# Turning joined with scoring, and the last stage's query factor and gate products rearranged, in a ten-stage transformer kernel

## The chip, the cores and the metric

The kernel runs on one core of one Trainium2 chip. The metric is the device time of one execution in microseconds (us). A measurement of a kernel is several executions; their median is given.

## The reference, cut to what matters

Two blocks are run one behind the other on 512 rows of width 1024, in float32. The first has two layers of a gated feed-forward, a mix of a short convolution and a forgetting attention over 8 heads of 64, a cross attention to 256 memory rows, and a second feed-forward. The second block is one layer of differential attention (8 heads, two score maps each) and one of stick-breaking attention with 16 heads of 64:

```python
z = jnp.einsum('bhqd,bshd->bhqs', qb, k).astype(jnp.float32) * scale
log_beta = jax.nn.log_sigmoid(z)
log_1mb = jnp.where(mask, jax.nn.log_sigmoid(-z), 0.0)
suffix = lax.cumsum(log_1mb, axis=3, reverse=True) - log_1mb
a = jnp.where(mask, jnp.exp(log_beta + suffix), 0.0)
...
proj = _rms(x, norm_g) @ w_in
q, g = jnp.split(proj, [SB_W], axis=-1)
o = _stick_breaking(q.reshape(b, s, SB_HEADS, SB_HEAD_DIM), k, v)
return x + (o.reshape(b, s, SB_W) * jax.nn.silu(g)) @ w_out
```

The norm of a row x is one factor per row, 1/sqrt(mean(x^2) + eps), times a gain per column.

## The kernel before

Ten stages follow one another: feed-forward, mix, cross attention, feed-forward, the same four again, `diff` and `sb` (the last). Activations stand as columns (128 features on the partitions, 512 rows along the free axis). Each matrix product is done in three passes for float32 accuracy: every operand is split into a high half (ScalarE, L1872 and L1875 for weights) and a low half (VectorE, L2255 for weights), and `mm3` (L1525 to L1527) issues low x high, high x low, high x high. A tile of 128 output features takes 8 such steps of 3 products of 512 columns. Weights come in blocks of 128x1024; in the last stage GpSimd first multiplies them by a gain (L2783).

The attention of a stage is laid into the projections. `att(n0, n1)` runs over n, where n = 4t + i is query block i (128 rows) of head pair t. A step of `bs`, `ms` or `ds` is the score product (L1770; six matmuls of 64 partitions into banks 4 and 5, over 128 x (i + 1) keys), with what follows on ScalarE and VectorE; a step of `bt` or `dt` turns the finished probabilities of block m = n - 2 (n - 3 in the last stage) by TensorE transposes (L1531; 2 x (i + 1) blocks into banks 6 and 7, in `diff` i + 1 blocks), after which ScalarE copies the high half (L2179) and VectorE subtracts the low half (`btl`, L2711; `dtl`, L2644). A turn waits for that subtraction of the turn before it. When all four blocks of a head pair are turned, the value products follow (`bpv`, L1811 and L1812; two per pair, one per pair in `diff`). Between steps the generator yields. `weave` advances this side stream by a fixed rate for each unit of 256 columns of the main stream: 10.5/80 means 10.5 side steps while 80 units of projection are issued. `later(5, ...)` puts a step on the other engines' order after 5 more units; `due` puts it there at once. One list, `order`, is the program order of every engine.

In the last stage a score becomes two sigmoids (ScalarE, L2170 with scale -1 and L2171), a reversed running product per head (VectorE scans, L2701), a masking product (L2705), and a product on GpSimd (L2889). Queries and keys are multiplied in their bank by RB, the rows' norm factors (VectorE, `bqe`, L2687), then copied (ScalarE, L2160) and subtracted (VectorE, `bql`, L2693). The output of a head pair stands in two banks, one per head, each in its own 64 partitions: `bps` (L2471) adds the half that `bpv` moved, `gy` (L2730) multiplies each half by the gate in ET, and L2187 and `gl` (L2736) split the result. The gate is made by `ga` (L2718), a sigmoid (L2183) and `gb` (L2723). In `diff`, column sums for the norms are small products (L1726, after ScalarE's squares L2097 and L2102; L1623, after L2145).

## Time and profile before

| | |
|---|---|
| Median of 3 runs (lowest, highest) | 2911.08 us (2909.06, 2913.7) |
| The profiled execution: its time, its span | 2911.05 us, 2909.2 us |
| Busy: TensorE, VectorE, ScalarE, GpSimd | 2843.3, 1676.3, 1092.2, 397.3 us |
| Mean granted TensorE clock | 0.995 of full |
| Instructions | 34967 |

The span goes from the first to the last instruction. Matmuls are pipelined, so their durations overlap and the start-to-start distance is what one costs. "Waits" name for each idle stretch of an engine the instruction that ended it.

### The profile page before, as it was taken

The numbers are of one execution on the slowest core, as the hardware profiler recorded it, in microseconds if no ns is written. First come the engines' busy times: TensorE is split into PE (matmuls) and PEld (weight loads), VectorE is DVE, ScalarE is ACT, GpSimd is POOL, SyncE is SP. The second block draws the span as 40 slices with busy tenths as digits, with TensorE's granted clock in tenths as the row PEclk, the third lists the DMA queues.
The fourth block names the chain that finished last, engine by engine and source line by source line (L and its number), as shares of the span: only waits on it lengthen the run. The fifth ranks groups of instructions, "written<-read, shape, count | busy, mean of one in ns | idle before, by whom it ended". The sixth has DMA issues, their size and how long they took to land.

```text
span 2909.2 us, 34967 instructions
## 1 busy us (share of the span) xinstructions
PE 2843.3 (98%) x14241; PEld 2363.5 (81%) x14241; DVE 1676.3 (58%) x2400; ACT 1092.2 (38%) x1699; POOL 397.3 (14%) x263
## 2 busy tenths in 40 slices
PE   8999999999999999999999999999999899899988
PEld 7888887888888888888887889888888787678777
DVE  5554357675464533555247776555533677768884
ACT  4322244554332322323234454422222444444442
POOL 2000111110100001000011220100001322154430
PEclk9999999999999999999999999999999999999999
DMA  4332332243233233332323233233323222131211
GB/s 141 101 95 94 95 88 73 66 127 106 87 94 97 88 101 98 101 95 87 105 71 92 68 108 118 80 109 95 101 91 98 70 64 69 47 88 59 72 59 51
DMA packets 302240, 258.08 MB, mean 89 GB/s; under 512 B 11367, under 2 KB 299904, under 8 KB 302080
## 3 DMA queue, kind: packets, MB, share of 16 engines
q1 hardware_dynamic: 300704, 254.76, 28.7%
q8 instruction: 113, 1.85, 0.3%
q10 hardware_dynamic: 1024, 1.05, 0.2%
q14 instruction: 47, 0.39, 0.0%
q0 software_dynamic: 352, 0.03, 0.0%
HBM read 252.66 MB, written 2.10 MB: 88 GB/s over the span
## 4 chain that ended last, share of the span: by engine, by line
PE 82%; DVE 10%; ACT 3%; issue 3%; POOL 2%; DMA 1%; ACTq 0%; SPq 0%; POOLq 0%; DVEq 0%
PE PS L1525 26%; PE PS L1527 25%; PE PS L1526 25%; DVE WL L2255 3%; PE PS L1531 2%; PE PS L1770 1%; DVE AF L2701 1%; DVE SM L2619 1%; ACT AF L2129 0%; PE PS L1623 0%; PE PS L1812 0%; PE PS L1811 0%; DVE AR L2711 0%; ACT WH L1872 0%; POOL SM L2869 0%
## 5 line engine op out<-in xcount | busy, mean ns | idle before, releaser
L2255 DVE TENSOR_TENSOR WL<-RAW,WH 128x1024 fp32r<-128x1024 f32 x480 | 617.9, 1293 | 572.9 <-ACT WH L1872 572.6
L1525 PE MATMUL PS<-XH,WL 128*128 128x512 f32 x2256 | 904.4, 401 | 2.9 <-DVE XL L2265 2.9
L1527 PE MATMUL PS<-XH,WH 128*128 128x512 f32 x2256 | 883.3, 392 | 0.0
L1526 PE MATMUL PS<-XL,WH 128*128 128x512 f32 x2256 | 882.1, 391 | 0.0
L1872 ACT ACTIVATE WH<-RAW 128x1024 fp32r<-128x1024 f32 x448 | 465.4, 1044 | 1005.9 <-PE PS L1527 994.6
L1525 PEld LDWEIGHTS PS<-XH,WL 128*128 128x128 f32 x2256 | 425.8, 189 | 101.5 <-issue 12.7
L1527 PEld LDWEIGHTS PS<-XH,WH 128*128 128x128 f32 x2256 | 425.2, 188 | 91.5
L1526 PEld LDWEIGHTS PS<-XL,WH 128*128 128x128 f32 x2256 | 426.3, 189 | 81.1
L1525 PE MATMUL PS<-AR,WL 128*128 128x512 f32 (+1 forms) x1216 | 465.3, 383 | 7.3 <-DVE SC L2599 3.5
L1527 PE MATMUL PS<-AR,WH 128*128 128x512 f32 (+1 forms) x1216 | 460.7, 379 | 0.0
L1526 PE MATMUL PS<-AR,WH 128*128 128x512 f32 (+1 forms) x1216 | 460.6, 379 | 0.0
L2805 POOL TENSOR_TENSOR SC<-SC 128x512 f32<-128x512 f32 x70 | 117.5, 1678 | 1619.3 <-ACT SC L1897 1614.7
L1525 PEld LDWEIGHTS PS<-AR,WL 128*128 128x128 f32 x1216 | 229.4, 189 | 52.0 <-issue 9.2
L1527 PEld LDWEIGHTS PS<-AR,WH 128*128 128x128 f32 x1216 | 229.2, 188 | 43.1
L1526 PEld LDWEIGHTS PS<-AR,WH 128*128 128x128 f32 x1216 | 229.4, 189 | 41.0
L1525 PE MATMUL PS<-WH,XL 128*128 128x256 f32 x384 | 113.3, 295 | 0.8 <-DVE AR L2693 0.8
L2324 DVE TENSOR_TENSOR AF<-PS,RB 128x512 f32<-128x512 f32 x88 | 60.4, 687 | 85.9 <-PE PS L1527 85.9
L1526 PE MATMUL PS<-WL,XH 128*128 128x256 f32 x384 | 109.1, 284 | 0.0
L1527 PE MATMUL PS<-WH,XH 128*128 128x256 f32 x384 | 109.0, 284 | 0.0
L2337 DVE TENSOR_TENSOR AR<-AF,AR 128x512 fp32r<-128x512 f32 x88 | 60.9, 692 | 61.7 <-ACT AR L1934 61.7
L2318 DVE TENSOR_TENSOR SC<-PS,RB 128x512 f32<-128x512 f32 x88 | 60.1, 687 | 59.1 <-PE PS L1527 45.6
L1934 ACT ACTIVATE AR<-AF 128x512 fp32r<-128x512 f32 x88 | 55.3, 628 | 98.5 <-DVE AF L2332 98.5
(259 smaller groups left out, 3000.0 us busy)
## 6 DMA issues: line engine op xcount, KB each, us to landing
RAW<-in_w_ffn_gu_dram SPq DMA_DIRECT2D x176, 512.0 KB, 3.5
RAW<-in_w_ffn_down_dram SPq DMA_DIRECT2D x80, 512.0 KB, 3.4
RAW<-in_w_mix_in_dram SPq DMA_DIRECT2D x48, 512.0 KB, 4.0
RAW<-in_w_xkv_dram SPq DMA_DIRECT2D x32, 512.0 KB, 3.4
RAW<-in_a_w_in_dram SPq DMA_DIRECT2D x32, 512.0 KB, 4.2
RAW<-in_w_mix_out_dram SPq DMA_DIRECT2D x16, 512.0 KB, 3.4
RAW<-in_w_xq_dram SPq DMA_DIRECT2D x16, 512.0 KB, 4.1
RAW<-in_w_xo_dram SPq DMA_DIRECT2D x16, 512.0 KB, 3.4
```

The source lines that it names most:

```text
L1525: pe.matmul(o, ll, rh, start=start, stop=False, skip_group_check=skip)
L1526: pe.matmul(o, lh, rl, start=False, stop=False, skip_group_check=skip)
L1527: return pe.matmul(o, lh, rh, start=False, stop=stop, skip_group_check=skip)
L1531: t = pe.transpose(PS[b][:, i * 128:(i + 1) * 128], src[:, i * 128:(i + 1) * 128], ID)
L1770: w = pe.matmul(PS[4 + hh][:, 0:N], QK[r, q, qs], QK[r, k, 0:N], start=q == sl + 1, stop=last and q == sl and k == sl + 2)
L1872: act.activation(h, src, ACT.Copy).then_inc(sg["wh"].up(n))
L1934: act.activation(AH[:, f, :], AF[:, (f % 2) * T:(f % 2) * T + T], ACT.Copy).then_inc(sg["fh"].up(s, f))
L2255: dve.tensor_tensor(l, raw_slot(n), F(h), ALU.subtract).then_inc(sg["wl"].up(n))
L2318: dve.tensor_tensor(S[f % 2], PS[C.banks[f % 2]][:, :], RB[:, :], ALU.mult).then_inc(sg["fs"].up(s, f))
L2324: dve.tensor_tensor(w, PS[C.banks[f % 2]][:, :], RB[:, :], ALU.mult).then_inc(sg["fu"].up(s, f))
L2337: dve.tensor_tensor(AL[:, f, :], AF[:, (f % 2) * T:(f % 2) * T + T], F(AH[:, f, :]), ALU.subtract).then_inc(sg["fl"].up(s, f))
L2805: pool.tensor_tensor(S[5], S[5], square_of(m), ALU.add).then_inc(sg["acc"].up(s, m))
```

## The change

Turning is joined with scoring: in the four attention stages the generator no longer yields between a turn and the score that follows it, and the rates of the side streams are set anew for the smaller number of steps. In the last stage the queries are taken from their bank without the norm factor; it goes in as the scale per row of the two sigmoids (RCOL, and NB4 = -RCOL, made once). `bps` of the second head writes into the bank of the first, so that one product of 128 partitions (`gy`) serves both heads, and the second bank is free once it is added.

```diff
@@ mix, att (the same in diff and sb with n >= 32)
                     self.add("bt", (s, m), "ptr", "ph")
-                    yield
+                    if n >= 16:
+                        yield
@@ mix
-        side = self.stream(att(0, 4), 6.5 / 64)
+        side = self.stream(att(0, 4), 4.3 / 64)
...
-            side = self.stream(att(4 * m, 4 * m + 4), 10.5 / 80)
+            side = self.stream(att(4 * m, 4 * m + 4), 6.3 / 80)
...
-        side = self.stream(att(12, 16), 10.5 / 80)
+        side = self.stream(att(12, 16), 6.3 / 80)
@@ diff
-            side = self.stream(att(4 * t, 4 * t + 4), 9.4 / (80 if t in (2, 4) else 48))
+            side = self.stream(att(4 * t, 4 * t + 4), 5.3 / (80 if t in (2, 4) else 48))
...
-        side = self.stream(att(28, 33), 10.4 / 33)
+        side = self.stream(att(28, 33), 6.3 / 33)
@@ due
+        if step[0] == "gy":
+            for hh in range(2):
+                self.due("bps", (LAST, *step[1], hh))
@@ heads_in
-        self.add("bqe", (s, w, t), "et", "eh")
+        self.add("bqe", (s, w, t), *(() if s == LAST and w == "q" else ("et",)), "eh")
@@ stick
-                self.give(b, "gy", (t,))
+                self.give(b, "bps", (s, t, 1))
...
-        self.add("mq", (s,), "mask", "zero", "tri")
+        self.add("mq", (s,), "mask", "zero", "tri", "minus")
...
-        side = self.stream(att(0, 4), 6 / 64)
+        side = self.stream(att(0, 4), 4.3 / 64)
...
-            side = self.stream(att(4 * t - 4, 4 * t), 10.5 / (32 + (32 if t % 2 else 0) + (16 if t < 7 else 0)))
+            side = self.stream(att(4 * t - 4, 4 * t), 6.3 / (32 + (32 if t % 2 else 0) + (16 if t < 7 else 0)))
...
-        side = self.stream(att(28, 33), 13 / 56)
+        side = self.stream(att(28, 33), 8.2 / 56)
@@ tensor, bpv
-                free[b] = [{"mix": ("yl", (s, t, hh)), "diff": ("dov", ("o", t)), "sb": ("gy", (t,))}[nm(s)]]
+                free[b] = [{"mix": ("yl", (s, t, hh)), "diff": ("dov", ("o", t)), "sb": ("pvs", (s, t, 1)) if hh else ("gy", (t,))}[nm(s)]]
@@ scalar, bqe: queries of the last stage wait for the product alone
-                on.wait_ge(*sg["et"].at(s, w, t))
+                if s == LAST and w == "q":
+                    on.wait_ge(*sg["mm"].at(((s, f"{w}{t}"), 0), 0, KT - 1))
+                else:
+                    on.wait_ge(*sg["et"].at(s, w, t))
@@ scalar, bs
-                act.activation(OM[n % 2][:, :, T - N:T], z, ACT.Sigmoid, scale=-1.0).then_inc(sg["exps"].up(s, n))
-                act.activation(BE[n % 3][:, :, T - N:T], z, ACT.Sigmoid).then_inc(sg["sbe"].up(s, n))
+                i = n % 4
+                on.wait_ge(*sg["minus"].at(s))
+                act.activation(OM[n % 2][:, :, T - N:T], z, ACT.Sigmoid, scale=NB4[:, i:i + 1]).then_inc(sg["exps"].up(s, n))
+                act.activation(BE[n % 3][:, :, T - N:T], z, ACT.Sigmoid, scale=RCOL[:, i:i + 1]).then_inc(sg["sbe"].up(s, n))
@@ vector, mq
+                    on.wait_ge(*sg["rcol"].at(s))
+                    dve.tensor_scalar(NB4, RCOL, -1.0, None, ALU.mult).then_inc(sg["minus"].up(s))
@@ vector, bps
-                y = PS[P.bank_of[s, t, hh]][r, :]
                 on.wait_ge(*sg["pvx"].at(s, t, hh))
-                dve.tensor_tensor(y, y, F(YL[r, t, :]), ALU.add).then_inc(sg["pvs"].up(s, t, hh))
+                dve.tensor_tensor(PS[P.bank_of[s, t, 0]][r, :], PS[P.bank_of[s, t, hh]][r, :], F(YL[r, t, :]),
+                                  ALU.add).then_inc(sg["pvs"].up(s, t, hh))
@@ vector, bqe
+                if s == LAST and w == "q":
+                    return
@@ vector, gy
-                for hh in range(2):
-                    r = slice(64 * hh, 64 * hh + 64)
-                    on.wait_ge(*sg["pvs"].at(LAST, t, hh))
-                    y = dve.tensor_tensor(ET[r, t % 2, :], ET[r, t % 2, :], PS[P.bank_of[LAST, t, hh]][r, :], ALU.mult)
-                y.then_inc(sg["gy"].up(t))
+                on.wait_ge(*sg["pvs"].at(LAST, t, 1))
+                e = ET[:, t % 2, :]
+                dve.tensor_tensor(e, e, PS[P.bank_of[LAST, t, 0]], ALU.mult).then_inc(sg["gy"].up(t))
```

## Rows read from the trace of the kernel before

**Rows 1.** The page's first part: busy us, share of the span, instructions.
```profile
PE 2843.3 (98%) x14241; PEld 2363.5 (81%) x14241; DVE 1676.3 (58%) x2400; ACT 1092.2 (38%) x1699; POOL 397.3 (14%) x263
```

**Rows 2.** Busy time by stretch (us; engines; clock, DMA): first mix, diff, last.
```profile
413.00:560.00 147.00, 145.19 (x790) 116.96 (x789) 110.42 (x193) 69.17 (x137) 27.68 (x21) 1.00 0.29 80
...
2285.00:2550.00 265.00, 249.08 (x1412) 199.26 (x1411) 195.13 (x425) 122.61 (x268) 54.95 (x36) 0.98 0.21 62
2600.00:2870.00 270.00, 251.17 (x1440) 205.19 (x1439) 218.04 (x282) 128.21 (x192) 106.29 (x58) 0.97 0.22 65
```

**Rows 3.** TensorE's waits in the last stage: total us, times, longest.
```profile
PE PS L1531 <- DVE AR L2711: 14.0, 7, 2.9
PE PS L1811 <- DVE AF L2723: 3.1, 1, 3.1
PE PS L1811 <- DVE AR L2711: 1.1, 1, 1.1
PE PS L1770 <- DVE AR L2693: 0.7, 1, 0.7
```

**Rows 4.** TensorE in order of time, last stage: two turns that waited.
```profile
2700.57 1.51 PE L1531 MATMUL PS<-IDR,SC 128*128 128x128 f32 x6 [2.52 <-DVE AR L2711]
...
2732.23 0.85 PE L1531 MATMUL PS<-IDR,SC 128*128 128x128 f32 x6 [1.66 <-DVE AR L2711]
```

**Rows 5.** VectorE, then GpSimd, in order of time before the turn at 2732.23.
```profile
2723.24 4.29 DVE L2701 TENSOR_TENSOR_SCAN AF<-AF,AR 128x512 f32<-128x512 f32 x2
...
2728.37 3.11 DVE L2255 TENSOR_TENSOR WL<-RAW,WH 128x1024 fp32r<-128x1024 f32 x1
2731.40 0.68 DVE L2711 TENSOR_TENSOR AR<-PS,AR 128x512 fp32r<-128x512 f32 x1
...
2727.99 2.41 POOL L2889 TENSOR_TENSOR SC<-SC,AF 128x1024 f32<-128x1024 f32 x1 [1.54 <-DVE SC L2705]
```

**Rows 6.** Groups of instructions: busy us, mean ns, idle before.
```profile
L2255 DVE TENSOR_TENSOR WL<-RAW,WH 128x1024 fp32r<-128x1024 f32 x480 | 617.9, 1293 | 572.9 <-ACT WH L1872 572.6
...
L2687 DVE TENSOR_TENSOR PS<-PS,RB 128x512 f32<-128x512 f32 x32 | 21.9, 694 | 8.2 <-PE PS L1527 8.0
...
L2730 DVE TENSOR_TENSOR AF<-AF,PS 64x512 f32<-64x512 f32 x16 | 11.0, 685 | 0.3
...
L1886 ACT ACTIVATE XH<-X x8: 615/632/636, 2569.0 to 2585.8; 128x512 fp32r<-128x512 f32 x8
...
L1888 ACT ACTIVATE XH<-X,GA x64: 706/710/727, 13.2 to 1886.5; 128x512 fp32r<-128x512 f32 x64
```

**Rows 7.** Busy time by stretch, behind the wait of 2.52 us.
```profile
2700.60:2703.80 3.20, 3.20 (x11) 2.81 (x12) 3.20 (x3) 1.21 (x2) 2.95 (x2) 0.50 0.52 169
2703.90:2707.10 3.20, 3.20 (x18) 2.26 (x18) 3.17 (x5) 2.25 (x4) 2.49 (x2) 1.00 0.00 0
```

**Rows 8.** TensorE in order of time: turn and score apart, then adjoining.
```profile
2694.02 0.60 PE L1531 MATMUL PS<-IDR,SC 128*128 128x128 f32 x4
...
2694.68 0.40 PE L1526 MATMUL PS<-XL,WH 128*128 128x512 f32 x1
...
2695.61 0.40 PE L1527 MATMUL PS<-XH,WH 128*128 128x512 f32 x1
2695.94 0.55 PE L1770 MATMUL PS<-AR 64*128 64x128 f32 x6
...
2305.70 0.66 PE L1531 MATMUL PS<-IDR,SC 128*128 128x128 f32 x4
2306.28 0.97 PE L1770 MATMUL PS<-AR 64*128 64x512 f32 x6
```

**Rows 9.** First mix stage in order of time: a score's last products, its last sums.
```profile
512.15 0.40 PE L1785 MATMUL PS<-AR 40*128 40x512 f32 x2
...
517.18 0.20 ACT L2003 ACTIVATION_READ_ACCUMULATOR SC<-PS,SM 128x1 f32 x1
```

**Rows 10.** TensorE's waits in the differential stage: total us, times, longest.
```profile
PE PS L1726 <- ACT SC L2102: 3.8, 4, 3.1
...
PE PS L1623 <- ACT SC L2145: 1.7, 2, 0.9
```

More of the change, by code:

```diff
@@ L863, in att @@
                     self.later(4, "dtl", (s, m), "pl")
-                    yield
+                    if n >= 32:
+                        yield
                 if n < 32:
@@ L1105, in att @@
                     self.later(5, "btl", (s, m), "pl")
-                    yield
+                    if n >= 32:
+                        yield
                 if n < 32:
@@ L2691, in bql @@
                 on.wait_ge(*sg["eh"].at(s, w, t))
-                on.wait_ge(*sg["et"].at(s, w, t))
+                if s < LAST or w == "k":
+                    on.wait_ge(*sg["et"].at(s, w, t))
                 dve.scalar_tensor_tensor(l, tile_bank(s, w, t), f, F(h), ALU.mult, ALU.subtract).then_inc(sg["el"].up(s, w, t))
```

## The prediction

> **What bounds the kernel now.** I read the page first. TensorE is busy for 2843.3 of 2909.2 us [rows 1], so only what shortens or fills TensorE's own time counts, and all its gaps together are 66 us. Then the stretches in which a turn or a score stands [rows 2]: a mix stage idles TensorE for 147 - 145.2 = 1.8 us, the differential stage for 265 - 249.1 = 15.9 us, the last stage for 270 - 251.2 = 18.8 us at a mean clock of 0.97. VectorE is busy for 218 of those 270 us, the fullest of the three. Then who ends the waits of the last stage [rows 3]: 14.0 us in seven waits of a turn (L1531) for the low-half subtraction (L2711) of the turn before it; 3.1 us of a value product (L1811) for the gate product L2723, which frees its bank; 0.7 us of the first score for the low half of queries or keys (L2693).
>
> Where the turns wait is seen in order of time. Six of the seven stand at the turn of six blocks, the third query block of a head pair; two are shown [rows 4], 2.52 and 1.66 us. The reason stands on VectorE before the second [rows 5]: the two scans of the widest score take 4.29 us, then a low half of weights 3.11 us instead of its mean 1.29 [rows 6], and only then, at 2731.40, comes the subtraction that the turn needs. The 3.11 us overlaps GpSimd's product of 2727.99 to 2730.40. That wait also costs clock: after the one of 2.52 us the granted clock is 0.50 (1.2 GHz), and 11 TensorE instructions start or run in 3.2 us, where the next 3.2 us at 1.00 (2.4 GHz) have 18 [rows 7]. Seven too few at 0.23 us each are 1.6 us. The last stage's 0.97 is 0.03 x 270 = 8 us of lost clock, so some four or five such stretches.
>
> The Trainium skill ("SBUF — State Buffer", Who interferes with whom) says that a VectorE instruction with two SBUF inputs and a reading GpSimd instruction block each other fully. The trace agrees with it in the 3.11 us above.
>
> **Part by part.** *Joining (all four stages).* 87 turns move to directly ahead of a score: 14 in each mix stage, 30 and 29 in the others (one pair adjoins already). No instruction is added or dropped. What the break itself costs is in [rows 8]. One step of a 512-column product is (2695.61 - 2694.68) / 4 = 0.23 us. A lone turn of four blocks takes 0.66 us to the second product behind it, less one step 0.43; a score's entry takes 0.33 instead of 0.23. Apart: 0.43 + 0.10 = 0.53 us. Joined, in the one case of the trace, the score starts 0.58 us after the turn's first instruction, which itself followed a short wait. So joining gains at most the 0.10 of the entry (-9 us over 87) and loses at most 0.05 (+4 us). I take 0, since the direct row is nearest to 0.53.
>
> What matters is the order. Before, a head pair has 10.5 shares of its stretch for 10 side steps, after it 6.3 for 6 (9.4 for 9 and 5.3 for 5 in the differential stage). From the second value product to the turn of six blocks there are 5/10.5 = 0.476 of a stretch before and 3/6.3 = 0.476 after: the turn is wanted at the same time. But the widest score comes after 1/6.3 = 0.16 in place of 2/10.5 = 0.19 of a stretch. A unit of 256 columns is three half steps, 0.345 us, so this is 0.5 us earlier in a stretch of 48 units and 0.9 us in one of 80. VectorE's 4.29 us of scans can start that much earlier.
>
> *Fewer VectorE products in the last stage.* Eight L2687 (the queries' half of them) at 0.69 us are 5.6 us, and eight of the 16 half-height L2730, which cost 0.69 us each at 64 partitions as at full height, are 5.5 us [rows 6]. Together 11 of 218 us. One L2730 lies in the chain ahead of each turn of six blocks. So each of the six waits shortens by 0.5 to 0.9 (score earlier) + 0.69 (product), less some 0.1 for slower sigmoids: 1.1 to 1.5 us, 1.3 on average, 7.8 us in all. Two of the three or so long ones fall to about 1.2 us and should keep the clock: -3.2 us. If the weights' low half still falls onto GpSimd's product, nothing of this is sure; that is a rival below.
>
> *Queries without the norm factor.* The first score waits 0.7 us [rows 3] for a chain in which the queries' product stood ahead of the keys': -0.7 us. *Bank freed by the add (bps)*: the value product that waited 3.1 us still needs the bank of the last gate tile, but one add is now ahead of its gate's products instead of between: -0.7 us.
>
> *Sigmoids with a scale per row.* 64 ScalarE instructions read a pointer. By L1888 against L1886, 710 against 632 ns for the same shape, that is 0.08 us each [rows 6], 5 us on ScalarE, 0.16 us per score. ScalarE is busy for 128 of 270 us and scores of this stage hardly wait; hidden, and if the cover is gone 32 x 0.16 = 5 us. The small product for the negated factor lies before the first score, within its 0.7 us.
>
> The Trainium skill ("ScalarE: Activation LUTs", What ACT_TABLE_LOAD costs) gives about 93 ns for each pointer operand, which speaks against this edit; by it the cost would be an estimated 6 us of ScalarE, as hidden as the 5.
>
> *New waits.* In the last stage a turn and a value product now follow the turn before them by one main stretch of 7.6 or 12.7 units (2.6 or 4.4 us) instead of two of 4.6 or 7.6 (3.2 or 5.3 us) with a score between. Behind a turn lie the copy, and VectorE with score work and perhaps a low half of weights (1.29 us). Bounds: 0, if VectorE has nothing else; 1.3 us for each of the seven value pairs and of seven turns of eight blocks, 18 us. Nearest is 0 in the long stretches and some 0.3 in the short ones: +1.5 us. For a mix stage the tight spot is the score after a score: from the last score product at 512.15 to the end of its exponentials 517.38 are 5.2 us [rows 9]; the next score comes after 0.33 + 4.4 + a turn of 0.4 = 5.1 us. Late by 0 to 0.3 us, seldom; with the value products' lesser distance I take +0.5 us per stage, +1.0.
>
> *Differential stage.* The column-sum product L1726 waits 3.8 us, 3.1 of it once, for ScalarE's squares, and L1623 1.7 us [rows 10]. The 3.1 is a tile whose square is queued on ScalarE behind the exponentials of the fourth score, which is the sixth step, at 6 x 48/9.4 = 30.6 units, while the tile ends at 32. After the change the fourth score comes at 4 x 48/5.3 = 36.2 units, behind the square in the queue, and what is ahead of it is the third, at 27.2: 3.4 units or 1.2 us earlier, and narrower. I take -1.5 us, and half a clock stretch, -0.8. L1623 follows a score by more, since a value product now comes 9.1 or 15.1 units after it instead of 5.1 or 8.5: -1.7. Scores closer to each other by 1.1 units: +0.5. Together -3.5 us.
>
> Sum: -7.8 - 3.2 - 0.7 - 0.7 + 1.5 (last stage, -10.9), -3.5 (differential), +1.0 (mix), 0 (break) = -13.4 us. The profiled execution took 2911.05 us, its span 2909.2; the median of the runs is 2911.08, so the same base serves. **2897.7 us**, 0.46% less.
>
> **The rivals.** *B: the waits stay.* The subtraction that the turn of six blocks needs is ordered a little later than before (5 units after the turn, which is the second step of 6.3 and not the third of 10.5), so the weights' low half may again come first and be blocked by GpSimd's product, as in [rows 5]; what VectorE saves ends as idle time elsewhere. Then -0.7 - 0.7 for the first score and the bank, -1.5 for waits shortened here and there, +1.5 new: 2909.6 us. For it: the 3.11 us depends on order, not on load. Against: 11 us less work on an engine that is busy for 218 of 270 us. The Trainium skill's rule above is on this rival's side: by it the block is full whenever the two meet, and one place of the trace agrees.
>
> *C: slower, by the value products and the turns of eight blocks.* They follow a turn after one main stretch. If VectorE is more than 2.6 us behind at those places (it decides from there), 14 waits in the last stage and 13 elsewhere (7 and 2 x 3) at 1.0 us, near the upper bound of 1.3, are +27 us in place of the 2.5 that I took: 2911.05 - 15.9 + 27 = 2922 us. For it: 4.29 us of scans show how far VectorE can fall behind. Against: before, the value products of the last stage wait for hardly more than the bank's 3.1 us [rows 3].
>
> *D: nearly all waits go.* The 14.0 us of turns, four clock stretches of 1.6, half of the 15.9 us of the differential stage and 2 us elsewhere are 30 us, 14.0 + 6.4 + 8 + 2: 2881 us. It needs the low half of weights to fall clear of GpSimd's product at all six places.
>
> **How the numbers follow.** My forecast (2890 to 2905.2) 0.55, B 0.19, C 0.13, D 0.13. The bounds of the unknown costs (-9 to +4, 0 to +18) lie within these. Leaving out a tenth below and a tenth above gives 2884 to 2912. No change is here within 0.2%, 2905.3 to 2916.9, about what a measurement of this kernel can tell. Faster: 0.55 + 0.13 + 0.02 of B = 0.70. Same: 0.17 of B + 0.01 of C = 0.18. Slower: 0.12 of C.
>
> **What would show it.** In the last stage, waits of turns for the low-half subtraction at 6 us or less instead of 14.0, at most two stretches at clock 0.50, TensorE idle about 10 us of the same 270, VectorE some 11 us less busy, sigmoids 0.08 us longer. In the differential stage, L1726's 3.1 us halved. In the mix stages, idle time up by under 1 us. The prediction is wrong if the turns of six blocks wait as before (B), or if value products and turns of eight blocks appear in the waits with over 5 us (C).

## The result, and the profile after

The changed kernel takes 2925.14 us in the median of 5 runs (2919.2 to 2927.55), and 2925.02 us in a second set of 5 on another occasion. Against runs of the kernel before on the same chip the ratios are 1.0044 [1.0031, 1.0057] and 1.0034 [1.0022, 1.0047]: slower by 0.3 to 0.4%, some 12 us. 2897.7 us was forecast, in a range from 2884 to 2912. The profiled execution took 2920.59 us, with a span of 2918.8; it is one of the faster of the five, so the stage times below show less of the loss (9.6 us of span) than the medians do (14 us).

The page's first part, of the kernel after:

```profile
PE 2843.5 (97%) x14241; PEld 2370.4 (81%) x14241; DVE 1682.3 (58%) x2385; ACT 1097.7 (38%) x1699; POOL 396.9 (14%) x263
```

TensorE is busy for the same 2843 us as in [rows 1]: in this execution the loss is all idle time. VectorE has 15 instructions fewer and yet 6 us more busy time, which comes back below.

Busy time by stretch, of the kernel after (length; busy us of TensorE, its weight loads, VectorE, ScalarE, GpSimd; clock, DMA share, GB/s): the differential stage, the last stage.

```profile
2283.00:2562.00 279.00, 249.77 (x1411) 202.43 (x1411) 203.01 (x426) 124.53 (x268) 56.18 (x37) 0.97 0.20 59
2612.00:2880.00 268.00, 249.62 (x1442) 204.94 (x1441) 214.86 (x268) 132.23 (x193) 105.69 (x59) 0.99 0.22 65
```

The first line says where the time went. The stretch holds the same 1411 or 1412 TensorE instructions as the one of [rows 2], is 14 us longer, and TensorE idles for 29 us of it, not 16. The stages' own lengths I take from the first product of a stage's norm sums (L1629) to that of the next. In order of time, of the kernel after (the first is the start of the differential stage, the second that of the last):

```profile
2253.25 0.28 PE L1629 MATMUL PS<-SM,SC 128*128 128x1 f32 x2
```

```profile
2607.48 0.27 PE L1629 MATMUL PS<-SM,SC 128*128 128x1 f32 x1 [1.00 <-POOL SC L2819]
```

That is 354.2 us for the differential stage. In the same way:

| us, one profiled execution each | before | after | forecast | measured |
|---|---|---|---|---|
| mix stages | 173.8, 173.4 | 171.9, 171.5 | +0.5 each | -1.9 each |
| differential stage | 339.4 | 354.2 | -3.5 | +14.8 |
| last stage | 313.8 | 311.3 | -10.9 | -2.5 |

TensorE's waits in the differential stage (2283 to 2562 us), the six largest, of the kernel after (total us, times, longest):

```profile
PE PS L1776 <- DVE AR L2621: 5.9, 4, 2.9
PE PS L1629 <- DVE SC L2616: 4.6, 4, 1.5
PE PS L1732 <- ACT SC L2108: 4.6, 4, 1.2
PE PS L1531 <- DVE SC L2612: 4.2, 1, 4.2
PE PS L1531 <- DVE AR L2657: 4.1, 4, 1.5
PE PS L1537 <- DVE AR L2657: 3.8, 3, 2.2
```

L1732 is the column-sum product L1726 of [rows 10]; in place of one wait of 3.1 us it has four of 1.1 to 1.2. L1629 (L1623 before) no longer waits for ScalarE's squares but, four times, for VectorE's product L2616, which frees bank 7. Value products (L1531 on L2657, 4.1 us) and turns (L1537, 3.8 us) wait for the low half of the last turn, and the first scores of a head pair (L1776) for the queries' low half. All waits of the whole stage, 2253 to 2607 us, are 34.1 us together; before they were 20.9.

In the last stage, of the kernel after:

```profile
PE PS L1537 <- DVE AR L2727: 8.2, 10, 2.1
PE PS L1817 <- DVE AR L2727: 8.2, 5, 2.1
PE PS L1817 <- DVE AF L2739: 1.1, 1, 1.1
PE PS L1537 <- DVE SC L2282: 0.9, 1, 0.9
```

Against [rows 3] the turns wait 8.2 instead of 14.0 us, and the value products for the same kind of low half 8.2 instead of 1.1.

### The profile page after: what moved, and what is told of

Same layout as the page of the kernel before. It is cut to its first block, busy times and chain, and to the rows that moved or that the text cites. A ratio compares the mean times of both kernels' runs of the same rounds, so it can differ in the third digit from the quotient of the medians.

```text
span 2918.8 us, 34950 instructions
## 1 busy us (share of the span) xinstructions
PE 2843.5 (97%) x14241; PEld 2370.4 (81%) x14241; DVE 1682.3 (58%) x2385; ACT 1097.7 (38%) x1699; POOL 396.9 (14%) x263
## 4 chain that ended last, share of the span: by engine, by line
PE 86%; DVE 7%; ACT 2%; issue 2%; POOL 1%; DMA 0%; ACTq 0%; SPq 0%; POOLq 0%; DVEq 0%
PE PS L1531 27%; PE PS L1533 26%; PE PS L1532 26%; DVE WL L2266 2%; PE PS L1776 2%; PE PS L1537 2%; DVE AF L2717 1%; DVE AR L2727 1%; PE PS L1818 1%; PE PS L1817 1%; PE PS L1629 1%; ACT AF L2135 0%; DVE SM L2632 0%; ACT WH L1878 0%; POOL SC L2827 0%
## 5 line engine op out<-in xcount | busy, mean ns | idle before, releaser
L2266 DVE TENSOR_TENSOR WL<-RAW,WH 128x1024 fp32r<-128x1024 f32 x480 | 625.4, 1308 | 575.1 <-ACT WH L1878 574.9
L1531 PE MATMUL PS<-XH,WL 128*128 128x512 f32 x2256 | 897.6, 398 | 2.9 <-DVE XL L2276 2.9
L1531 PEld LDWEIGHTS PS<-XH,WL 128*128 128x128 f32 x2256 | 425.8, 189 | 104.6 <-issue 12.6
L1531 PE MATMUL PS<-AR,WL 128*128 128x512 f32 (+1 forms) x1216 | 465.0, 382 | 7.8 <-DVE SC L2612 4.2
L1531 PEld LDWEIGHTS PS<-AR,WL 128*128 128x128 f32 x1216 | 229.4, 189 | 52.1 <-issue 9.9
L1531 PE MATMUL PS<-WH,XL 128*128 128x256 f32 x384 | 112.7, 293 | 0.0
```

The source lines that it names most:

```text
L1531: pe.matmul(o, ll, rh, start=start, stop=False, skip_group_check=skip)
L2266: dve.tensor_tensor(l, raw_slot(n), F(h), ALU.subtract).then_inc(sg["wl"].up(n))
```

## The experiments

Sixteen runs were made, one of them of the changed kernel again, each against the kernel before. A ratio carries an interval of about 0.1% either way, so differences under some 3 us between two medians of ten runs, and under 4 to 5 us where one has five, are not told apart. "Expected" is what was written down before each run.

Stage times are of one execution each, and repeats of the same order differ. For the differential stage, of which every kernel has the same 1801 or 1802 TensorE instructions:

| order of the stage, run | stage us | TensorE idle | TensorE busy | mean clock |
|---|---|---|---|---|
| as before: before, e1 | 339.4, 343.6 | 22.7, 22.4 | 316.7, 321.2 | 0.98, 0.97 |
| as changed: after, e10, e4 | 354.2, 356.1, 362.7 | 35.1, 34.4, 36.1 | 319.1, 321.7, 326.6 | 0.97, 0.96, 0.95 |

The idle time repeats within 2 us; the busy time of the same instructions is 7.5 us longer in e4 than in the kernel after, at a lower granted clock. So a stage time alone does not rank two orders that lie within some 8 us; the idle time does better, and the time of the whole kernel is judged by its median.

### Which part of the change costs

**e1_diff_apart**: the changed kernel, the differential stage as before.

```diff
                     self.later(4, "dtl", (s, m), "pl")
-                    if n >= 32:
-                        yield
+                    yield
...
-            side = self.stream(att(4 * t, 4 * t + 4), 5.3 / (80 if t in (2, 4) else 48))
+            side = self.stream(att(4 * t, 4 * t + 4), 9.4 / (80 if t in (2, 4) else 48))
...
```

> The changed kernel with turning and scoring apart again in the differential stage alone (its old yield and its old rates, 9.4 and 10.4). Theory 1, the loss lies in the differential stage, whose part of the trace grew from 339.4 to 354.2 us: this kernel is 14.8 us faster than the changed one, some 2905 to 2909 us, and the differential stage takes 339 us again. Rival, what is lost there is only carried over from what stands before it (weights that arrive later): the stage still takes over 345 us and the kernel stays above 2915.

Measured: 2905.66 us, ratio 0.9976 [0.9967, 0.9985]; 0.24% faster than before. The differential stage took 343.6 us.

**e2_last_sums_only**: the kernel before with the last stage's arithmetic alone (scale in the sigmoids, one gate product), no turn joined.

> The kernel before with the last stage's queries' factor in the sigmoids and the single gate product, and no joining anywhere. Theory 1, 11 us less work of VectorE shorten the seven waits of turns: 3 to 8 us faster than before, 2903 to 2908 us. Rival, the waits are set by order and not by load: within 2 us of 2911, VectorE 11 us less busy and more idle.

Measured: 2910.37 us, 0.9996 [0.9987, 1.0006]: no change that could be told, as the rival had it. TensorE's waits in the last stage (2598 to 2910 us), of this kernel:

```profile
PE PS L1534 <- DVE AR L2724: 14.0, 7, 3.0
...
PE PS L1814 <- DVE AR L2724: 1.1, 1, 1.1
```

The turns wait 14.0 us in seven waits, exactly as in [rows 3]. VectorE's busy time in the stage went from 232.5 to 227.2 us, 5 us less and not 11; the weights' low halves took the rest (below).

**e3_sums_and_mix**: the same with the mix stages' turns joined.

> The kernel of the single gate product and the queries' factor, with joining in the two mix stages alone. Theory 1, each mix stage gains the 1.8 to 2.0 us that the two traces differ by there: 3 to 4 us faster than the kernel with the sums alone. Rival, that difference was chance or came from the stage before: the same time as it within 1 us.

Measured: 2908.57 us, 0.9984 [0.9975, 0.9994], between the two guesses; mix stages 171.9 and 171.5 us, as in the kernel after.

**e4_joins_only**: all four joins on the kernel before, old arithmetic.

> Joining in all four stages with the new rates, and the last stage's arithmetic as before. Theory 1, in the last stage joining trades the turns' waits for waits of the value products, so without the saved VectorE work it is slower there by some 5 us than the changed kernel: 2928 to 2934 us. Rival, the last stage's arithmetic does nothing: 2925 us as the changed kernel.

Measured: 2921.66 us, 1.0035 [1.0022, 1.0048], below both guesses. TensorE's waits in the last stage (2615 to 2923 us), of this kernel:

```profile
PE PS L1534 <- DVE AR L2714: 10.5, 10, 2.1
PE PS L1814 <- DVE AR L2714: 6.2, 5, 1.5
```

The last stage took 309.2 us, no longer than the changed kernel's 311.3 and 311.1.

What follows: joining in the differential stage costs 19.5 us (2925.14 - 2905.66), a difference of the two ratios says the same (1.0044 - 0.9976 = 0.0068, 19.8 us). That is more than the whole loss. The rest is small: joining in the last stage gives 2.9 us (2908.57 - 2905.66), in the mix stages 1.8, the arithmetic alone 2.6 (2912.94, the kernel before beside it, - 2910.37), and with the turns joined the arithmetic shows no gain (e4 against the changed kernel). Each of these lies within what two medians can tell.

### Why the differential stage loses

Laid side by side, the two orders differ in more than the joining. A tile ends after 16 units (8 steps of 3 products) of a stretch, and its squares are then ordered on ScalarE. Joined steps stand every 9.06 units in a stretch of 48 and every 15.1 in one of 80, so in the long stretches a step falls at 15.1 and one at 30.2, each just ahead of a tile's end as the order is written: the tile's last product is issued, then the joined step, and only then the tile's own work for the other engines. The score's two exponentials then stand ahead of the squares in ScalarE's order. Here is what that does. ScalarE in order of time, of the kernel after (start, us, engine and line; in brackets the idle time before and what ended it):

```profile
2353.82 0.46 ACT L2135 ACTIVATE AF<-PS,SM 128x128 f32<-128x128 f32 x1 [2.17 <-DVE SM L2637]
...
2354.27 0.45 ACT L2135 ACTIVATE AF<-PS,SM 128x128 f32<-128x128 f32 x1
...
2354.70 0.59 ACT L2103 ACTIVATE SC<-PS 128x512 f32<-128x512 f32 x1
2355.18 0.69 ACT L2108 ACTIVATE SC<-PS,GB 128x512 f32<-128x512 f32 x1
```

and TensorE, of the same kernel:

```profile
2355.92 1.05 PE L1732 MATMUL PS<-SM,SC 128*128 128x2 f32 x8 [1.23 <-ACT SC L2108]
```

The tile had ended before the score at 2351.20. ScalarE was idle for 2.17 us, because its next instruction was the exponential, which waits for VectorE's row maxima (L2637); the squares behind it (L2103) could have run at once, as f1 below shows. The column sums then wait for the second pass over the tile (L2108), which follows the squares.

**e5_don_early** tries the other order that changed, on bank 7.

```diff
-            self.later(4, "don", ("o", t), "don", "dos", "dop")
+            self.later(2, "don", ("o", t), "don", "dos", "dop")
```

> The changed kernel, with the sums of squares of the value product (don) put 2 units behind the value product instead of 4, so that in a stretch of 48 units they stand ahead of the key's factor (dkt) on TensorE, as they do in the kernel before. Theory A (order among the small steps): the four waits of L1629 for VectorE L2616, 4.6 us together, go; the differential stage 354.2 -> about 349.6 us, the kernel 2925.1 -> about 2920.5. Theory B (the joined step is too tight whatever stands around it): the waits turn up at the next line; 2924 to 2926. Theory C: the value product's squares (ScalarE) are not ready two units behind it, and TensorE waits for them instead: 2926 to 2929.

Measured: 2915.69 us, 1.0011 [1.0002, 1.002]; 9.4 us better than the changed kernel, twice what was expected. L1629's waits for L2616 are gone, and the stage's waits sum to 28.7 us. The one profiled execution shows 353.1 us for the stage: its idle time is 29.9 us, 5 us less than the changed kernel's, its busy time 323.2, 4 us more. So the size rests on the medians (11 runs here, 5 of the changed kernel) and is good to some 5 us either way.

**e6_steps_later** moves every joined step of the stage one or two units later.

```diff
             side = self.stream(att(4 * t, 4 * t + 4), 5.3 / (80 if t in (2, 4) else 48))
+            side[2] = -0.15
```

> The changed kernel, with every stretch of the differential stage started at a count of -0.15 instead of 0, so that each joined step stands one to two units later and behind the end of the tile it fell just ahead of; the squares of that tile are then ordered on ScalarE ahead of the score's exponentials. Theory A: the four waits of L1732 for ScalarE L2108 (4.6 us) go, and in the stretches of 48 units the value product's small steps come ahead of the key's too, which takes the waits of L1629; the stage 354.2 -> 345 to 350 us, the kernel 2925.1 -> 2916 to 2921. Theory B (tight coupling): 2924 to 2926, the waits only change their line.

Measured: 2906.42 us, 0.9978 [0.9969, 0.9988], 10 us below what the better guess had; differential stage 342.6 us, waits 24.6. The four waits of L1732 are gone, and the first scores' wait for the queries' low half fell too, from 5.9 to 1.7 us. Not all went as expected: L1629's waits for the key's factor only fell to 3.0 us, and the turns' for the low half of the last turn rose from 3.8 to 6.1. One number of this size gives back 18.6 us, about all of the joining's cost. Joining at every place is thus not bound to lose.

**e8_values_later** gives the value product one more piece of main work behind the last turn.

```diff
                         self.due("evl", (((s, f"v{(m - 4) // 8}"), 0), i))
+                    if n < 32:
+                        yield
                     values_of(m // 4 - 1)
...
-            side = self.stream(att(4 * t, 4 * t + 4), 5.3 / (80 if t in (2, 4) else 48))
+            side = self.stream(att(4 * t, 4 * t + 4), (6.3 if t else 5.3) / (80 if t in (2, 4) else 48))
```

> The changed kernel, with one more, empty step in each stretch of the differential stage between the tile's last turn and its value product (rate 6.3 instead of 5.3): the value product then has one more piece of main work ahead of it, and the joined steps stand closer, 7.6 units apart instead of 9.1 in a stretch of 48. Theory B (tight coupling of the value product to the last turn): the four value products' waits for L2657 (4.1 us) go, the kernel 2925.1 -> about 2921. Theory A (order and place of the small steps): the value product's small steps come later still and meet the key's; 2925 to 2930.

Measured: 2946.31 us, 1.0115 [1.0102, 1.0129], far above both guesses; the stage 380.5 us. The steps are closer by 16%, and TensorE's waits sum to 48.7 us; the mean clock falls to 0.989. The value products' wait for the low half is gone, as expected, and more came elsewhere, most of all 12.8 us of turns that wait for the low half of the turn before (3.8 in the changed kernel).

**e11_half_steps** keeps the distances of the kernel before: a joined step counts as two, a value product as one, at the old rate of 9.4.

```diff
                     self.later(6, "dc", (s, n), "prob")
+                    if n > 1:
+                        yield
                     yield
...
-            side = self.stream(att(4 * t, 4 * t + 4), 5.3 / (80 if t in (2, 4) else 48))
+            side = self.stream(att(4 * t, 4 * t + 4), 9.4 / (80 if t in (2, 4) else 48))
...
```

> The changed kernel, but in the differential stage a joined turn and score count as two steps and a value product as one, at the rates of the kernel before (9.4 instead of 5.3 to a stretch): turns stand as far apart as before (10.2 units in a stretch of 48, not 9.1) and only the score is moved, to directly behind its turn. Theory S (spacing: the value product took a whole joined step, so turns came 11% closer and met the bank's low half): the waits on L2657 (7.9 us) and on the query's low half (5.9 us) fall, stage 354 -> 343 to 348 us, kernel 2908 to 2915. Theory P (place against tile ends alone): this layout still has the key's squares ordered just behind a score's exponentials, but don ahead of dkt; stage 348 to 352. Theory J (joining as such): 352 to 356.

Measured: 2932.2 us, 1.0065 [1.0053, 1.0078]; the stage 370.0 us, waits 36.0, clock 0.989. All three guesses were too low, and the spacing theory falls for this stage: turns and value products stand where they stood before, only the scores come earlier, and the stage is slower still. L1734, the column sums, waits five times for the pass behind the squares (4.5 us). The largest wait (2283 to 2562 us) is another one:

```profile
PE PS L1539 <- DVE SC L2672: 9.6, 5, 2.3
```

L2672 is the copy on VectorE that prepares the value output's row factor, which TensorE then turns (L1539). In the whole stage this wait is 11.1 us, against 2.5 in the changed kernel and 4.0 before. At 2344.44 us, where TensorE waits 2.32 us for it, it stands in VectorE's order behind a score's additions and maxima. It looks like a third case of the same kind, but no run moved this copy alone.

**e10_changed_again** and **e13_steps_later_still** (`side[2] = -0.3`):

> The changed kernel as it is, a second time, beside the next three on the same chip: 2920 to 2928 us, differential stage 353 to 355, last stage 309 to 311.

> The changed kernel with every stretch of the differential stage started at a count of -0.3 instead of the -0.15 that gave 2906.42 us. By the theory of places (what matters is on which side of a tile's end a joined step stands, not how far) the squares stay ahead of the exponentials and the time is that of -0.15 within 3 us: 2904 to 2910. If the gain of -0.15 came from the distance itself, or was chance, the time goes on down or back up: below 2902 or above 2914.

Measured: 2925.02 us for e10, with 356.1 us for the differential and 311.1 us for the last stage; and 2916.75 us, 1.0015 [1.0006, 1.0023], for e13. Twice the shift gives 8 us in place of 19; the expected plateau isn't there. The stage's waits sum to 27.4 us, and one of 2.8 us of the column sums for the squares is back. So it is not enough that a step stands behind a tile's end, places matter to a unit or two, and -0.15 was partly luck.

**f1_squares_first** leaves all of TensorE's places as they are and changes ScalarE's order alone.

```diff
...
-            yield from self.tile(((s, f"{w}{t}"), 0), b)
+            for i, y in enumerate(self.tile(((s, f"{w}{t}"), 0), b)):
+                if i == 7:
+                    self.due("dlo", (w, t - 1))
+                    self.add("dsq", (w, t), "dsq", "dg")
+                yield y
```

(The squares are then not ordered again at the tile's end; everything that is counted from there stays.)

> The changed kernel, with the two ScalarE passes of a tile (its squares and its scaled copy) put in ScalarE's order one matmul of the tile earlier, so that they stand ahead of the exponentials of a score that falls just ahead of the tile's end; TensorE's order and places are those of the changed kernel. Theory Q (order on ScalarE's queue): the four waits of L1732 for ScalarE (4.6 us) go and with them part of the queries' low halves that come late (5.8 us); stage 354 to 356 -> 345 to 351 us, kernel 2914 to 2920. Theory D (distances): exponentials behind the squares make the probabilities late instead; 2923 to 2928.

Measured: 2914.74 us, 1.001 [1.0001, 1.0019], as theory Q had it, the stage 349.7 us. ScalarE at the same place, of this kernel:

```profile
2349.91 0.58 ACT L2108 ACTIVATE SC<-PS 128x512 f32<-128x512 f32 x1
2350.39 0.68 ACT L2113 ACTIVATE SC<-PS,GB 128x512 f32<-128x512 f32 x1
...
2352.53 0.46 ACT L2140 ACTIVATE AF<-PS,SM 128x128 f32<-128x128 f32 x1 [1.09 <-DVE SM L2642]
```

and TensorE's column sums (L1737 here):

```profile
2353.28 0.95 PE L1737 MATMUL PS<-SM,SC 128*128 128x2 f32 x8
```

The squares (L2108) now run 2.6 us ahead of the exponential (L2140), and the column sums start with no wait. The stage's idle time is 31.1 us, 4 us less than the changed kernel's. This order alone is worth 10.3 us by the medians (11 runs against 5), again to some 5 us either way.

**f2_both_orders** adds the order of e5, and spaces the last stage as in e12 below.

> The same, with the value product's sums of squares 2 units behind it (ahead of the key's factor, as in the kernel before), and the last stage spaced as in the run where it took 305.8 us. Theory Q: L1629's 4.0 to 4.6 us go as well; differential stage 341 to 346 us, last stage 304 to 308, kernel 2901 to 2908. Theory D: differential stage 350 or more, kernel 2912 or more.

Measured: 2905.07 us, 0.9973 [0.9963, 0.9983], as theory Q had it; the differential stage 345.4, the last 308.6 us. TensorE's waits in the differential stage (2283 to 2562 us), of this kernel:

```profile
PE PS L1783 <- DVE AR L2628: 6.1, 4, 2.9
PE PS L1538 <- DVE SC L2619: 4.2, 1, 4.2
PE PS L1544 <- DVE AR L2664: 3.9, 3, 2.2
PE PS L1538 <- DVE AR L2664: 3.8, 5, 1.5
PE PS L1544 <- DVE SC L2677: 1.9, 2, 0.9
...
```

The column sums' and L1629's waits are out of the list; the waits for low halves (6.1, 3.9 and 3.8 us) are what they were. The stage's idle time is 25.0 us: of the 12.4 us that the change had added, 10.2 are gone.

### The last stage

**e9_last_values_later** puts an empty step between last turn and value products there, on top of e1.

```diff
+                    if n < 32:
+                        yield
                     for hh in range(2):
                         values_of(m // 4 - 1, hh)
                         yield
...
-            side = self.stream(att(4 * t - 4, 4 * t), 6.3 / (32 + (32 if t % 2 else 0) + (16 if t < 7 else 0)))
+            side = self.stream(att(4 * t - 4, 4 * t), (7.3 if t > 2 else 6.3) / (32 + (32 if t % 2 else 0) + (16 if t < 7 else 0)))
```

> The changed kernel with the differential stage's turns and scores apart (2905.66 us as run before), and in the last stage an empty step between a tile's last turn and its two value products (7.3 instead of 6.3 steps to a stretch). Rival C's mechanism: the five waits of L1817 for L2727 (8.2 us) fall to under 2 us, and the joined steps, 8.8 -> 7.6 units apart in a stretch of 64, add less than 3 to the turns' 8.2 us; about 2900 (2898 to 2903). Against it: the low halves come late because VectorE and ScalarE are behind as a whole, and the waits only move to the turns and scores; 2905 to 2908.

Measured: 2912.91 us, 1.0003 [0.9995, 1.0012], above both guesses; the last stage 317.8 us. TensorE's waits there, of this kernel:

```profile
PE PS L1538 <- DVE AR L2728: 18.9, 10, 4.1
...
```

The value products' 8.2 us are gone, and the turns' went from 8.2 to 18.9. The first half of the expectation held, the price was over three times as high (10.7 us more for the turns, where less than 3 was expected): with turns 14% closer together, each waits for the low half of the one before, which frees their bank.

**e12_late_and_half**: joined everywhere, e5 and e6 together, and in the last stage a joined step counted as two, a value product as one.

```diff
                     self.later(5, "bmul", (s, n), "gprob")
+                    if n > 2:
+                        yield
                     yield
...
-            side = self.stream(att(4 * t - 4, 4 * t), 6.3 / (32 + (32 if t % 2 else 0) + (16 if t < 7 else 0)))
+            side = self.stream(att(4 * t - 4, 4 * t), 10.5 / (32 + (32 if t % 2 else 0) + (16 if t < 7 else 0)))
...
```

> Joined everywhere: the differential stage with steps one to two units later (as in the run of 2906.42 us) and don 2 units behind the value product; in the last stage a joined step counts as two and each value product as one (rate 10.5), so that turns stand 12.2 units apart in a stretch of 64 again and not 10.2. By the spacing theory the last stage's waits of turns and value products (16.4 us) fall by a third or more, its time 310.6 -> 305 to 309 us; the differential stage loses the 3.0 us of L1629, 342.6 -> about 340; kernel 2898 to 2904. If spacing has no part, the last stage stays at 309 to 312 and the kernel at 2904 to 2907.

Measured: 2909.61 us, 0.999 [0.9981, 0.9999], above the expected 2898 to 2904. The last stage took 305.8 us as expected, the differential stage 350.1 against the expected 340. With the steps later, the value's sums 2 units behind their product fall directly behind the key's factor on bank 7 and wait 5.3 us: the two remedies do not add.

**f3_apart_and_half** and **f4_late_and_half_alone** set the spaced last stage on e1 and on e6.

> Differential stage with turns and scores apart (343.6 us as run before), last stage joined with a joined step counted as two and a value product as one (305.8 us as run before): the two stages' times simply add to a kernel of 2900 to 2903 us. If the last stage's gain hung on what stood ahead of it, 2904 to 2908.

> Joined in all stages; differential stage one to two units later with the sums of squares where the changed kernel has them (342.6 us as run before), last stage spaced (305.8 us): 2899 to 2904 us. It tells, beside the run that also had the sums 2 units behind the value product (350.1 us), what that move alone costs at these places: 5 to 8 us.

Measured: 2902.87 us, 0.9968 [0.9955, 0.998], last stage 307.4 us; and 2907.2 us, 0.9977 [0.9967, 0.9986], last stage 306.1 us. TensorE's waits in the last stage, of f3:

```profile
PE PS L1538 <- DVE AR L2728: 6.6, 6, 1.9
PE PS L1818 <- DVE AR L2728: 6.2, 4, 1.9
PE PS L1818 <- DVE AF L2740: 2.9, 1, 2.9
```

f3 is as expected, f4 is not (2899 to 2904). The spaced last stage took 305.8 to 308.6 us in four kernels, the joined one without spacing 308.7 to 311.3 in nine executions: some 3 us by the profiles, but by the medians 2.8 on e1 and nothing on e6; the size stays open. f4 was also to tell what the value's sums 2 units behind their product cost at e6's places: 7.5 us by the stage (350.1 against 342.6), 2.4 by the medians, so that stays open too. f3 has the lowest median of all, 8 to 9 us below the kernel before, though e1, e6, f2 and f4 lie within its interval or at its edge.

## Why the prediction was wrong

**What bounds the kernel: right.** In the profiled execution TensorE's busy time did not move by a microsecond, and all of the loss is idle time. Where the granted clock falls, the busy time of the same 14241 instructions grows with it: 2856.2 us in e11, at a mean of 0.989.

**The break costs 0: within its bounds, and small.** The mix stages, where the join was forecast to cost 0.5 us each, gain 1.9, and e3 against e2 gives 1.8 for both together by the medians. Fourteen turns at the 0.10 us of an entry that I named as the most to gain would be 1.4. The waits seen there fell from 2.6 to 1.4 us, and that of 0.3 us for a score behind a score does not appear. In the first mix stage TensorE's idle time fell by 1.3 us and its busy time by 0.6, which is 0.04 us for each of 14 turns. No run kept the two apart.

**The last stage, -10.9: two terms were mis-sized, and a part of one failed.**

- Turns' waits: -5.8 (14.0 to 8.2) where -7.8 stood. Clock: its stretch went from 0.97 to 0.99, and the stretches at 0.50 from four to two, at 1.7 us each (the granted clock summed in steps of 0.8 us) -3.4, where -3.2 stood. First score: its 0.7 us are gone. Bank: 3.1 to 1.1 us, -2.0 for -0.7.
- New waits: the value products' went from 1.1 to 8.2 us, +7.1, and 0.9 us of a turn for L2282 is new. +1.5 had been taken, from a range up to 18. This is rival C's mechanism, at its named place, in five waits of up to 2.1 us. The sum of the measured terms is -5.8 - 3.4 - 0.7 - 2.0 + 7.1 + 0.9 = -3.9, beside -2.5 for the stage.
- "One L2730 lies in the chain ahead of each turn of six blocks", 0.69 us of each wait: this part failed. With the arithmetic alone (e2) the turns' waits stayed at 14.0 us. With the joins alone (e4) they fell to 10.5, with both to 8.2, and what the arithmetic took from the turns (2.3) the value products gained (6.2 to 8.2). All waits of both kinds for the last turn's low half together are 15.1, 15.1, 16.7 and 16.4 us, in the order before, e2, e4, after. So the turns' -5.8 comes mostly with joining, and no run shows the product's 0.69 us as time.
- The 11 us that VectorE was to save did not reach it in full. Its busy time in the last stage went from 232.5 to 227.2 us with the arithmetic alone, and from 235.9 (e4) to 228.5 with the turns joined. The rest is in the weights' low halves. The group of instructions in the last stage, of the kernel before, of e2, of e4 and of the kernel after (busy us, mean ns, idle before):

```profile
L2255 DVE TENSOR_TENSOR WL<-RAW,WH 128x1024 fp32r<-128x1024 f32 x36 | 56.1, 1577 | 0.5 <-ACT WH L1872 0.5
```

```profile
L2263 DVE TENSOR_TENSOR WL<-RAW,WH 128x1024 fp32r<-128x1024 f32 x36 | 60.9, 1709 | 0.5 <-ACT WH L1875 0.5
```

```profile
L2258 DVE TENSOR_TENSOR WL<-RAW,WH 128x1024 fp32r<-128x1024 f32 x36 | 66.7, 1866 | 0.5 <-ACT WH L1875 0.5
```

```profile
L2266 DVE TENSOR_TENSOR WL<-RAW,WH 128x1024 fp32r<-128x1024 f32 x36 | 66.8, 1867 | 0.5 <-ACT WH L1878 0.5
```

The same 36 instructions cost 10.7 us more in the changed kernel, and 10.6 us more with the joins alone: it is the new order that puts them beside GpSimd, and the arithmetic alone also adds 4.8. Sorted by whether a GpSimd instruction overlaps them for over 0.4 us, 16 of 36 do before, at a mean of 2.02 us, and 22 after, at 2.26; the others take 1.22 and 1.24. The Trainium skill ("SBUF — State Buffer", Who interferes with whom) says that such a pair block each other, and the trace agrees: 2.0 to 2.3 us beside GpSimd against 1.2 without. That is rival B's mechanism for the arithmetic: the waits go by order, not by VectorE's load, and e2 shows it.
- A count in the working is off without effect: from the second value product to the turn of six blocks there are 5.5/10.5 and 3.3/6.3 of a stretch, 0.52 each, since half a step is left over at a stretch's end; the two are still equal.

**The sigmoids' scale: right.** The four widths take 84 to 97 ns more each (1020 to 1116 ns at the widest), where 0.08 us was taken; no wait of TensorE in the last stage names them, and VectorE's idle time ahead of its scans fell from 8.5 to 6.2 us.

**The differential stage, -3.5: this is the step that failed.** It said that the fourth score at 36.2 units would come behind the square in the queue, and "what is ahead of it is the third, at 27.2". That was worked for the stretch of 48 units, where the one long wait stood. It did cure that wait: the 3.1 us are gone. The prediction did not place the steps of the other rate, 15.1 units in the stretches of 80, against the tiles' ends at 16 and 32. There each tile's squares went behind a score's exponentials, four new waits of 1.1 to 1.2 us. It also laid the value's sums only against their own score ("-1.7", which did come: they no longer wait for the squares), and not against the key's factor at 31 units, which uses the same bank; value product at 27.2 + 4 comes behind it, at 25.5 + 4 before. That is 4.6 us. And low halves come late: the queries' for the next pair's first score, 5.9 instead of 2.7 us, the last turn's for value products, 4.1 instead of 0, and for turns, 3.8 instead of 0.5. These three are 10.6 of the 13.2 us by which the stage's waits grew. The clock, -0.8 in the sum, went the other way: the busy time of the same instructions is 2.4 us longer.

f1 and e5 show the first two to be causes, at 10.3 and 9.4 us of the kernel's time. That is about two times the idle time that they remove (4.0 and 5.3 us). The other half fits with the clock: over all runs the mean granted clock is 0.9924 for the changed kernel, 0.9940 for f1 and e5, 0.9949 for e6 and 0.9947 for e1. 0.0016 of 2925 us is an estimated 4.7 us for f1 and for e5. For e1 it is 6.7 us beside 12.7 us less idle time, 19.4 of the 19.5 us. So of what joining costs here some two thirds are TensorE's idle time and a third is lower clock that comes with it. That the waits cause the lower clock was not tested by itself.

With both orders mended the joined stage is at 345.4 us, and in e6 at 342.6, where two executions of the order before took 339.4 and 343.6: by the stage no loss can be told for e6, and its median is 0.8 us from e1's. The waits for low halves, the near places of value product and turn, are rival C's 4.1 and 3.8 us. Of these, the turns' stay in every joined version (3.7 to 12.8 us), and the value products' are gone only in e8 and e11, which are slower.

**Rival C** was given 0.13 and 2922 us by 27 us of waits at value products and turns of eight blocks. The time came near (2925) partly by luck, since the cause is only in part this one: value products wait 8.2 us in the last stage, value products and turns 7.9 us in the differential stage, 16 of the 27. The other waits come from the order in two queues, which no rival had.

## What to carry to other kernels

When a side stream's rate is changed, write out the place of every step against the events of the main stream (tile ends, small products on a shared bank), for each length of stretch that the stream runs in; a step that falls one product earlier changes who is first in an in-order queue. A kernel in which one number, -0.15 of a step, moves 19 us has a cost that belongs to no single edit: try the neighbouring values before an edit is judged by its time. Work spared on an engine is worth something only if it lies in the chain that ends a wait; here the arithmetic alone left the turns' waits at 14.0 us, because they went by the order of the queue. Look at what runs in its place, and beside which other engine.

## What the runs showed that was not expected

- An exponential that waited for its maxima held ScalarE idle for 2.17 us with ready squares behind it; reordering only that saved 10.3 us in a kernel of 2925 us.
- The granted clock is a cost of its own, and no sum of waits gives it. The profiled executions of e8 and e11 ran at a mean of 0.989, where the changed kernel had 0.994: 0.005 x 2932 = 15 us, and in e11 that is about all of the stage's +15.8 us, since its waits sum to 36.0 against 34.1 us. In e4, with the changed kernel's order in this stage and 35.0 us of waits, the stage took 8.5 us longer, 7.5 of them busy time. In the last stage, stretches at 0.50 (1.2 GHz) stand behind waits of 2.1 to 3.1 us, yet not behind each: of the changed kernel's value products that waited 2.1 us, one has such a stretch behind it and two have none.
- Spacing acts in opposite ways in two stages of one kernel: turns at the old distances took the last stage to 305.8 to 308.6 us from 311.3, and the differential stage to 370.0 from 354.2 (there with the scores at new places, so distance is not the only thing that moved).
